# One residual block in fp32r on one core: each 512-column matmul with stationary weights written as two of 256 columns

## What is computed

```python
h = rmsnorm(x, g_mix)
proj = h @ w_in          # forgetting attention q, k, v, forget logits; LRU; memory q; 3 gates
...
branches = jnp.stack([y_fox, y_lru, y_mem], axis=2)
y_d = jnp.einsum('bsnc,ncd->bsnd', branches, w_branch)
gates = jax.nn.sigmoid(gate_logits.reshape(b, s, N_BRANCH, D_MODEL) + b_gate)
merged = jnp.sum(gates * y_d, axis=2)
x = x + merged @ w_out
up = causal_depthwise_conv(rmsnorm(x, g_ffn) @ w_ffn_up, w_ffn_conv, b_ffn_conv)
u_act, u_val = jnp.split(up, 2, axis=-1)
return x + (jax.nn.gelu(u_act) * u_val) @ w_ffn_down
```

## Time and profile before

| | |
|---|---|
| median of 3 runs | 1662.53 us (1662.39 to 1663.37) |
| span of the profiled execution | 1661.6 us |
| what the median has beyond that span | 0.9 us |
| TensorE busy with matmuls | 1641.6 us, 9356 matmuls |
| TensorE loading weights | 1426.6 us, 9356 loads |
| VectorE, ScalarE, GpSimd busy | 1117.1, 895.9, 54.9 us |
| mean DMA rate | 185 GB/s |

### The profile page before, as it was taken

One profiled execution on the slowest core, in us unless ns is written; L12 is line 12 of the kernel. 1 busy time (PEld: TensorE's weight loads), 2 busy tenths in 40 slices (PEclk: granted clock), 3 DMA queues, 4 the chain that ended last, 5 costly groups with the idle time before them and its releaser, 6 DMA issues.

```text
span 1661.6 us, 27207 instructions
## 1 busy us (share of the span) xinstructions
PE 1641.6 (99%) x9356; PEld 1426.6 (86%) x9356; DVE 1117.1 (67%) x1324; ACT 895.9 (54%) x1145; POOL 54.9 (3%) x57
## 2 busy tenths in 40 slices
PE   7999999999999999999999999999999999999998
PEld 6888888888888888888888888888888888888887
DVE  6977677678847566575666777777777777544443
ACT  6766567466644544545455555555555555434332
POOL 0010112000000000000001000000000000000000
PEclk9999999999999999999999999999999999999999
DMA  8544456553555555555565555555555655655653
GB/s 301 195 151 162 150 172 200 188 167 126 177 185 185 191 187 190 189 189 190 177 192 189 176 190 200 189 179 189 192 178 185 202 189 186 201 197 196 202 195 102
DMA packets 85833, 307.37 MB, mean 185 GB/s; under 512 B 9944, under 2 KB 11232, under 8 KB 85664
## 3 DMA queue, kind: packets, MB, share of 16 engines
q1 hardware_dynamic: 84672, 302.89, 55.0%
q0 software_dynamic: 1120, 3.94, 0.8%
HBM read 304.69 MB, written 2.11 MB: 185 GB/s over the span
## 4 chain that ended last, share of the span: by engine, by line
PE 94%; DVE 2%; issue 2%; ACT 1%; DMA 1%; SPq 0%; POOL 0%; ACTq 0%; DVEq 0%; POOLq 0%
PE psG L315 91%; PE psM L315 2%; DVE fox_rstd L910 1%; DVE W L885 1%; DMA mem_raw<-memT 0%; ACT W L554 0%; DMA lru_rg<-w_rg 0%; PE psM L406 0%; ACT fox_rstd L593 0%; DVE fox_S L938 0%; DVE stat L941 0%; DVE fox_q_n L926 0%; ACT L554 0%; ACT fox_S L583 0%; ACT fox_S L605 0%
## 5 line engine op out<-in xcount | busy, mean ns | idle before, releaser
L315 PE MATMUL psG<-X,W 128*128 128x512 f32 (+1 forms) x5632 | 993.2, 338 | 0.0
L315 PEld LDWEIGHTS psG<-X,W 128*128 128x128 f32 x5632 | 860.4, 188 | 128.1 <-issue 2.4
L885 DVE TENSOR_TENSOR W<-raw,W 128x1024 fp32r<-128x1024 f32 x567 | 687.8, 1227 | 314.9 <-ACT W L554 312.2
L554 ACT ACTIVATE W<-raw 128x1024 fp32r<-128x1024 f32 x567 | 591.2, 1054 | 318.7 <-PE psG L315 314.6
L315 PE MATMUL psG<-hidden,W 128*128 128x512 f32 (+1 forms) x1408 | 245.4, 337 | 0.0
L315 PEld LDWEIGHTS psG<-hidden,W 128*128 128x128 f32 x1408 | 214.0, 188 | 31.3
L562 ACT ACTIVATE low<-psG 128x512 f32<-128x512 f32 x140 | 83.8, 598 | 224.6 <-PE psG L315 224.6
L315 PE MATMUL psG<-Y,W 128*128 x768 | 134.4, 337 | 0.0
L315 PEld LDWEIGHTS psG<-Y,W 128*128 128x128 f32 x768 | 117.0, 188 | 17.1
L1300 DVE SCALAR_TENSOR_TENSOR up_c<-up_pad,par_sb,up_c 128x256 f32<-128x256 f32 x176 | 77.5, 482 | 42.3 <-ACT up_c L829 36.3
L315 PE MATMUL psG<-merged,W 128*128 128x512 f32 (+1 forms) x512 | 89.3, 337 | 0.0
(11 more groups left out here) (185 smaller groups left out, 672.5 us busy)
## 6 DMA issues: line engine op xcount, KB each, us to landing
raw<-w_units SPq DMA_DIRECT2D x567, 512.0 KB, 3.4
xs<-xT SPq DMA_DIRECT2D x4, 512.0 KB, 9.8
outT<-xs POOLq DMA_DIRECT2D x7, 256.0 KB, 3.6
mem_raw<-memT SPq DMA_DIRECT2D x3, 512.0 KB, 9.0
lru_rg<-w_rg POOLq DMA_DIRECT2D x8, 128.0 KB, 4.3
c_all<-c_rows POOLq DMA_DIRECT2D x1, 1024.0 KB, 8.8
mem_raw<-memT SPq DMA_DIRECT2D x4, 128.0 KB, 2.5
raw<-w_units SPq DMA_DIRECT2D x2, 256.0 KB, 3.2
```

The lines of the kernel that those rows point to most:

```text
L315: return nc.tensor.matmul(*a, skip_group_check=True, **kw)
L554: nc.scalar.activation(W[:, s, :, 0], raw[:, s], ACT.Copy).then_inc(hi_done, 1)
L885: V.tensor_tensor(W[:, s, :, 1], raw[:, s], f32(W[:, s, :, 0]), ALU.subtract).then_inc(lo_done, 1)
```

## The change

In `group`, for phases with stationary weights, the one matmul of 512 columns is written as two of 256 columns with the same stationary tile: the first over the high tokens into columns 0 to 255 of the bank, the second over the low tokens into columns 256 to 511. All else stays.

```diff
                             else:
-                                mm(psG[:, b + t, :], W[:, s, k, 0, ts], x_hl, start=kt == 0, stop=False)
+                                mm(psG[:, b + t, 0:T], W[:, s, k, 0, ts], x_hl[:, 0], start=kt == 0, stop=False)
+                                mm(psG[:, b + t, T:], W[:, s, k, 0, ts], x_hl[:, 1], start=False, stop=False)
```

## The result

| | before | after |
|---|---|---|
| median | 1662.83 us (4 runs) | 1713.57 us (4 runs, 1713.52 to 1713.79) |
| ratio | | 1.0303, 95% interval 1.0288 to 1.0317 |
| span of the profiled execution | 1661.6 us | 1712.1 us |
| TensorE's matmuls and loads | 9356 and 9356 | 13644 and 13644 |

The change makes the kernel 3.0% slower, 50.7 us. The forecast was 1654.6 us with a range of 1645 to 1680, so it had the sign wrong and the time lies outside.

The account below looks back on a forecast made before the run. TensorE's unbroken matmul stream was taken as the bound. Streaming took 7.9 us off the 1661.6 us span, loads and address instructions cost nothing, giving 1653.7; with 0.9 us beyond the span, 1654.6 us, range 1645 to 1680.

Parts of the forecast that it names:

- address instructions: Sequencer in branch: 96 more, hidden beside running matmuls; 6.5 us at most if nothing hides them.
- how the 696.7 ns divide between the shapes: One k-step of TensorE's stream: 233 ns between 512s, 115 between 256s, 349 for the two changes of shape.
- streaming term: TensorE's matmuls in 2144 k-steps: six at 115.5 ns make 693.0 ns, 3.7 less than now; 7.9 us less.
- upper bound: Streaming cost: from fp32 matmuls into psM, a fixed cost up to 4 ns per matmul, 17.2 us more.
- Rival 2: TensorE's stream: a fixed cost of 1 to 4 ns per matmul, 1679.7 us at 4 ns; chance 0.20.
- Rival 3: TensorE's weight loads: handing over tiles bounds each step at 0.12 us, 50 us more, 1712.5 us; chance 0.11.
- rule of the Trainium skill: TensorE, start to start: columns at 2.4 GHz plus about 2.5 ns per matmul; 10.7 us more, 1673.2 us.
- Rival 4: TensorE's added weight loads: not overlapped at all, 110 ns each, 472 us more, 2134 us; chance 0.01.
- rival 5: Second matmul of a pair: gets no load, stream costs the same, seen only in the load count; no chance given.
- wrong in kind: Sign for the whole forecast: the clock drops or a wait on `lo_done` appears.
- at its upper level all along: TensorE's clock in the kernel before: claimed to be at 2.4 GHz throughout.

Follow-up runs that it names:

- narrow_before: The kernel before with stationary tiles of 40 of 128 columns, except in branch and each group's first k-step; 1676.0 us, ratio 1.0081.
- alternate: The kernel before with each k-step ordered 512, 256, 512, 256 instead of 512, 512, 256, 256; 1668.1 us, ratio 1.0030.

## Why the prediction was wrong, point by point

- **Right:** TensorE's stream is the bound; 4288 more matmuls and as many loads; no new wait in the stream before the turn of down; address instructions and other engines cost nothing; branch at the same pace as up.
- **Wrong: the step that failed is "how the 696.7 ns divide between the shapes".** I took the distance from a 512 to the next 512 (233 ns) and from a 256 to the next 256 (115 ns) for what each costs. Run alone they cost 226.7 and 120.0. In a mix, starts are shifted within the pattern: the 512s look dearer and the 256s cheaper than they are. From 233 = 2 x 115 + 3 followed the idea that a 256 has no fixed cost; truly 2 x 120.0 - 226.7 = 13.3 ns, for each of 4288 splits. The streaming term, put at 7.9 us less, measured 50.0 us more. Only sums over whole periods can be trusted.
- **The better reading stood in the same rows.** Over a whole k-step, 696.7 less 1536 / 2.4 = 640 leaves 56.7 ns, 14.2 for each of four matmuls. At the forget logits 346.9 - 320 = 26.9, 13.5 for each of two, with tiles of only 40 columns. Two stretches with different loads gave nearly one number, though for the 40 columns with some luck: in the mix of `narrow_before` such tiles take 176.0 ns per matmul in up, 16.0 beside the columns. At 13.3 ns the sum would have been 4288 x 0.0133 = 57 us, against 50 measured, since the kernel before also lost 3.4 ns per k-step by its mix of widths (56.7 instead of 53.3), which the uniform kernel does not.
- **The upper bound was wrong too.** It came from fp32 matmuls, 216 ns for 256 columns. Those have some 3 ns beside twice their columns at 2.4 GHz; fp32r has 13.3. A row of another data type was no bound.
- **Rival 2 had the mechanism and the sign**, at 4 ns instead of 13.3, and for the upper clock level only. **Rival 3 had the time** by coincidence: its 0.12 us was read from one start distance, and a full 256 does take 120.0. But its mechanism, loads handed over at 120 whatever moves beneath, was refuted by the 240 columns at 112.5 ns.
- **The rule of the Trainium skill** (TensorE: Matmul & The Clock Gate, Back-to-back issue gap), columns at 2.4 GHz plus a fixed cost, had the right form, though that section gives it for matmuls taken without their loads, and I set it aside because a 512 seemed to take 233 ns instead of 216. Its 2.5 ns are near what the fp32 rows show, and a fifth of what fp32r shows here.
- **Rival 4 and rival 5** did not occur: loads overlap, and each matmul has one.
- **Small misses:** instruction transfers grew by 20, not ten, and they were put at nothing; the turn of the loop down cost 4.0 us once, 2.4 of pause and the rest at the lower clock. So the clock did drop, which the prediction had named as a sign of being wrong in kind, but as a consequence of the pause and for few of the 50.7 us. And "at its upper level all along" read the earlier trace rows too finely: each digit stands for 41 us, and in the first 19 us of the kernel before the clock was at its lower level part of the time.

What stays open: what the 13.3 ns are. At the lower clock level they are gone (214 ns for 256 columns). At the upper one they come with each matmul and its load, and these two were never separated: no run has an fp32r matmul without a load. They don't follow the load's length (9.4 ns with 96-column tiles under 256s, 16.8 under 512s), nor the bank or tile that came before. Why mixes of the same matmuls run at 173.3, 174.2 or 176.7 ns is open too, and `alternate` shows two of these with one order. There is one trace of each kernel, so whether a phase keeps its pace from run to run is not shown. Another data type was not tried.

## What to carry to other kernels

Where TensorE streams without a pause, work out its cost per matmul as the time of a whole period less its columns at the granted clock, divided by the matmuls in it; never from the distance between two neighbours of one shape in a mixed stream. In fp32r at the upper clock level that cost is 13 ns here, 6% of a 512 and 11% of a 256. So keep moving operands at 512 columns, and join matmuls with the same stationary tile rather than split them. Two runs with other sizes (one up, one down) would have told the law before the change was made.

## What the runs showed of the hardware that was not expected

- At a granted clock of 1.00 an fp32r matmul with a full 128-column tile took columns / 2.4 GHz + 13.3 ns at 256, 320, 384 and 512 columns, if all are of one width; with 240 and 192 columns it took 112 ns.
- At a granted clock of 0.50 the 13.3 ns are gone: 14 matmuls of 256 columns in 3.00 us, where 256 / 1.2 is 213.3 ns.
- A mixed stream has no single pace: the same order of matmuls ran at 176.7 ns each in one part of a kernel and at 173.3 in another.
- Tiles of 96 columns instead of 128 made 256-column matmuls 3.9 ns faster and 512-column ones 3.4 ns slower.
